# Prompt attention whose results stay in channel rows, with row factors applied in the merge

## The chip, the core and the metric

The kernel runs on one core of a Trainium2 chip. The metric is the device time of one execution in microseconds (us), start to end, for one step of a decoder layer on a prompt of 2048 tokens and 8 sequences of 8 new tokens each. PE is the matrix engine (PEld its weight loads), DVE the vector engine, ACT the scalar engine, POOL the general engine, SP the engine whose queue issues most transfers. PSUM is the memory that PE writes to, in 8 banks of 512 floats per partition; SBUF is the large on-chip memory of 128 partitions.

## The reference, cut to what matters

A layer normalises its input, projects it once, runs two token mixers side by side (a retention and a latent attention), multiplies each by a gate, projects both, adds them under two more gates and projects once more. The part that the change touches is the latent attention of the prompt and what follows it:

```python
def attend(args):
    qblk, start = args
    s = jnp.einsum('bqhd,bkhd->bhqk', qblk, k).astype(jnp.float32) * scale
    s = jnp.where(kpos[None, :] <= qpos[:, None], s, -jnp.inf)
    p = jax.nn.softmax(s, axis=-1).astype(v.dtype)
    return jnp.einsum('bhqk,bkhv->bqhv', p, v)
...
mla_o = mla_mixer(q_nope, q_pe, c_kv, k_pe, w_uk, w_uv) * jax.nn.silu(g_m)
p_mla = mla_o @ w_br_mla
merged = jax.nn.sigmoid(mg_r) * p_ret + jax.nn.sigmoid(mg_m) * p_mla
y = x + merged @ w_out
```

There are 8 heads with 64 value channels each (512 channels in all), 2048 positions, and query tiles of 128 rows. The softmax divides each row by the sum of its exponentials; that division can be done before or after the product with the values.

## The kernel before

The program has four stages, one after the other: `front` (projections and retention), `decode` (the new tokens), `attend` (prompt attention) and `merge` (gates, the two branch projections, the output projection, the norm). Every float is carried as a high and a low part for PE (`hi`, `lo`), and a product takes three matmuls (`three`, L66 to L68). All engines run their own hand-written list of instructions and wait for each other on counting semaphores; nothing is reordered.

**`attend`.** The loop goes over pairs of heads, and in a pair over 16 steps, 64 steps in all. A step handles two query tiles, a short one (`e` = 0) and a long one (`e` = 1), which together always have 17 blocks of 128 keys; the blocks are handled in 5 groups of up to 4. Step `g` works on three steps at once: scores of step `g`+1, transposes and most value products of step `g`, and the last two groups of values of step `g`-1. A group goes through these stages:

- `scores(j)` (PE): the product of queries and keys into bank j, plus the causal mask (L1881) on the diagonal block.
- `peak(j)` (DVE, L1812): the row maximum of the group; after a tile's last group, the maximum over its groups (L1816) and its negative (L1819, `nm`).
- `exps` (ACT, L1767): the exponentials, with their row sums in `total`.
- `turn(j)` (PE, L1889): the transposes, into bank 5 or 6.
- `high(j)` (ACT, L1754) and `low(j)` (DVE, L1802): the two parts of the transposed block, back into SBUF.
- `values(g, j)` (PE, L1900): values times probabilities into bank 7. The weights are the high and the low part of the values side by side (128 rows), and the moving data the high and the low part of the probabilities (256 columns). So bank 7 holds, for each of the two tiles, four partial sums: two halves of the partitions times two halves of the columns.

The four partial sums are added by PE. When `values(g-1, 4)` is done, ACT copies bank 7 into `ot` (L1773, "oc"); `folded()` multiplies it with a stacked identity (`fold`, L1910), which adds the partitions and turns the result to rows of tokens; DVE multiplies that with the reciprocals of the row sums (`result()`, L1837) into `out`. The row sums are added and inverted in `sums()` (L1826, L1829) in each step. `values(g, 0)`, the first to write to bank 7 again, waits for `result()`. SP stores `out` once per pair of heads to `OA` in DRAM (L1724), in rows of tokens. POOL has a task of its own: it loads the branch weights in 8 pieces and splits them into high and low parts (L1739 to L1743), as fast as they come.

PE's list for a step is, with the lines of the calls left out: scores(0), values(g-1,3), scores(1), values(g-1,4), turn(0), scores(2), turn(1), folded(), scores(3), turn(2), values(g,0), values(g,1), scores(4), turn(3), values(g,2), turn(4). DVE's: peak(0), peak(1), sums(), low(0), peak(2), result(), low(1), peak(3), low(2), peak(4), low(3), low(4). ACT's: oc, high(0), high(1), exps of tile 0, high(2), high(3), the first exps of tile 1, high(4), the other exps.

**`merge`.** It goes over 8 blocks of 256 tokens (the last also takes the 64 new tokens). SP's `main(n)` loads the inputs of block n into single buffers, as soon as the branch products of block n-1 are done. `turn(n)` (PE, L2171) transposes the block of `OA` back into channels, 8 transposes into banks 0 and 1; DVE multiplies them with the gate (`gated`, L2128), ACT and DVE split the product (L2092, L2130) into `ao`. For blocks after the first this runs between the first and the second token tile of the output projection of the block before. The branch products then take, for each of 8 channel groups k, 12 matmuls of the retention branch and 12 of the attention branch; only the latter need `ao`. In block 0 the output weights are still loaded and split on the way (L2105, L2144).

Of the kernel before, what the change touches and what calls it, by code (L numbers as in the profile page):

```python
# [1631 lines left out]
def attend(nc, T, early):  # L1632
# [7 lines left out]
    with ExitStack() as ctx:  # L1640
        sb, ps, sem = kit(nc, ctx)
        ident, hide, one_r = sb("t_ident", [P, P]), sb("t_hide", [P, P], F32R), sb("t_one_r", [P, P], F32R)
        hide_raw = sb("t_hide_raw", [P, P])
# [6 lines left out]
        total, den, rinv = sb("t_total", [P, 2, NGR]), sb("t_den", [P, 2, 2]), sb("t_rinv", [P, 2, 2])  # L1650
        ot = sb("t_ot", [P, 2, 2 * P])
        fold = sb("t_fold", [P, VD])
        out = sb("t_out", [P, 2, TILES, 2 * VD])
        w_raw = sb("t_w_raw", [P, 1, D_MODEL])
        bk = ps("t_bank", [P, 8, 512])
# [5 lines left out]
        by_group, by_tile, by_step = "qk mxs ex tp hi lo".split(), "red nm".split(), "dn rc pv oc of out".split()  # L1661
# [4 lines left out]
        w_in, w_high, w_low = sem("t_w_in"), sem("t_w_high"), sem("t_w_low")  # L1666
        block = ctx.enter_context(nc.Block())
# [23 lines left out]

        def over(eng, step):
# [11 lines left out]
        def _(sp):  # L1704
# [3 lines left out]
            sp.dma_start(hide_raw[:], T["hide"]).then_inc(consts, 16)  # L1708
# [11 lines left out]
            def store(r):  # L1720

                step_done(sp, "out", r, PAIR - 1)
                c = ds(2 * VD * r, 2 * VD)
                sp.dma_start(T["OA"][:, c].rearrange("(t p) n -> p t n", p=P), out[:, r % 2]).then_inc(stored, 16)  # L1724

            load(0)
            for r in range(1, NH // 2):
                load(r)
                store(r - 1)
            store(NH // 2 - 1)  # L1730
            sp.wait_ge(stored, 16 * (NH // 2))

        @block.gpsimd
        def _(g):
            g.wait_ge(consts, 32)
            g.tensor_copy(hide[:], hide_raw[:]).then_inc(ready, 1)
            g.tensor_copy(one_r[:], ident[:]).then_inc(ready, 1)
            for i, (w, src, c) in enumerate(early):
                g.dma_start(w_raw[:], T[src][c * P:(c + 1) * P, :].rearrange("(a p) n -> p a n", p=P)).then_inc(w_in, 16)  # L1739
                g.wait_ge(w_in, 16 * i + 16)  # L1740
# [3 lines left out]
                g.wait_ge(w_low, i + 1)  # L1744

        @block.scalar
        def _(a):
            def step(r, g, first, mid, last):
# [510 lines left out]
```

## Time and profile before

| what | us |
|---|---|
| median of 3 runs (2715.28 to 2720.17) | 2719.64 |
| the profiled execution | 2721.65 |
| its span, first to last instruction | 2719.9 |
| `front` and `decode`, to the start of `attend`'s transfers | 1722 |
| `attend`, first scores to the last result | 1746 to 2290 |
| `merge`, first transfer to the end | 2297 to 2720 |
| PE busy over the span | 2543.8 (94%) |
| DVE busy | 1462.3 (54%) |
| ACT busy | 1082.5 (40%) |
| POOL busy | 580.2 (21%) |

The profiled execution took 2721.65 us, of which 1.75 lie outside its span; it is 2.0 us above the median. Busy shares over the whole span mix stages with different limits. A row of the timeline has the start in us, the length, the engine, the line, what it writes and reads, and in brackets how long the engine had been idle before it and what it then waited for. Consecutive rows of one engine may overlap by a little, because a next instruction starts while the last one drains.

### The profile page before, as it was taken

How to read it: one execution, taken by the hardware profiler on the slowest of the kernel's cores; microseconds unless marked ns; L12 is line 12 of the kernel's file. 1: busy time of each engine (PE TensorE's matmuls, PEld its weight loads, DVE VectorE, ACT ScalarE, POOL GpSimd, SP SyncE). 2: the span in 40 equal slices, each digit the busy share in tenths (PEclk: the TensorE clock that was granted, in tenths of full speed). 3: DMA queues.
4: the chain of work that ended last, by engine and by line, in shares of the span. 5: the costliest groups of instructions: out<-in, count | busy, mean ns of one | idle time of the engine just before them, and what ended most of it. 6: DMA issues, size and time to landing. Idle time of an engine off the chain costs nothing. (4 is left out here: it accounts for less than half of the span.)

```text
span 2719.9 us, 44356 instructions
## 1 busy us (share of the span) xinstructions
PE 2543.8 (94%) x15981; PEld 2257.6 (83%) x15981; DVE 1462.3 (54%) x2772; ACT 1082.5 (40%) x2351; POOL 580.2 (21%) x446
## 2 busy tenths in 40 slices
PE   6999999999999999999789998499999997899998
PEld 6999987788878887788678887488888886799987
DVE  3345543355434554355368887288888885323232
ACT  3234331234313433233256664177777774211111
POOL 0023212124002320124115555130000000232322
PEclk9999999999999999999889998599999998899999
DMA  6677765778667876567344340632333202443431
GB/s 178 190 192 219 207 203 166 201 213 228 207 197 199 225 214 184 155 179 205 106 176 131 124 132 1 162 80 70 79 69 82 69 15 87 155 155 125 158 120 56
DMA packets 470443, 402.20 MB, mean 148 GB/s; under 512 B 50577, under 2 KB 419346, under 8 KB 463058
## 3 DMA queue, kind: packets, MB, share of 16 engines
q1 hardware_dynamic: 466690, 386.51, 50.2%
q10 hardware_dynamic: 2384, 8.65, 0.9%
q0 software_dynamic: 1152, 4.19, 0.5%
q8 instruction: 129, 2.11, 0.3%
q14 instruction: 88, 0.72, 0.1%
HBM read 297.82 MB, written 139.18 MB: 161 GB/s over the span
## 5 line engine op out<-in xcount | busy, mean ns | idle before, releaser
L66 PE MATMUL a_bank<-a_h_hi,a_w_hi 128*128 128x512 f32 (+3 forms) x1680 | 608.8, 362 | 20.8 <-DVE a_w_lo L755 15.8
L68 PE MATMUL a_bank<-a_h_hi,a_w_lo 128*128 128x512 f32 (+3 forms) x1680 | 596.4, 355 | 0.0
L67 PE MATMUL a_bank<-a_h_lo,a_w_hi 128*128 128x512 f32 (+3 forms) x1680 | 596.3, 355 | 0.0
L66 PEld LDWEIGHTS a_bank<-a_h_hi,a_w_hi 128*128 128x128 f32 (+1 forms) x1680 | 315.9, 188 | 67.8 <-DVE a_w_lo L755 19.0
L68 PEld LDWEIGHTS a_bank<-a_h_hi,a_w_lo 128*128 128x128 f32 (+1 forms) x1680 | 315.4, 188 | 44.3
L572 ACT ACTIVATE a_w_hi<-a_w_raw 128x1024 fp32r<-128x1024 f32 x168 | 175.0, 1043 | 436.7 <-PE a_bank L68 278.1
L67 PEld LDWEIGHTS a_bank<-a_h_lo,a_w_hi 128*128 128x128 f32 (+1 forms) x1680 | 316.1, 188 | 38.8
L755 DVE TENSOR_TENSOR a_w_lo<-a_w_raw,a_w_hi 128x1024 fp32r<-128x1024 f32 x168 | 205.7, 1225 | 207.5 <-ACT a_w_hi L572 207.5
L1802 DVE TENSOR_TENSOR t_pt<-t_bank,t_pt 128x512 fp32r<-128x512 f32 (+3 forms) x320 | 195.0, 610 | 73.0 <-ACT t_pt L1754 70.5
L1754 ACT ACTIVATE t_pt<-t_bank 128x512 fp32r<-128x512 f32 (+3 forms) x320 | 171.2, 536 | 134.8 <-PE t_bank L1889 134.2
L1767 ACT ACTIVATE t_prob<-t_bank,t_nm 128x512 f32<-128x512 f32 (+3 forms) x320 | 197.1, 628 | 37.3 <-DVE t_nm L1819 36.3
L1812 DVE TENSOR_REDUCE t_mx<-t_bank 128x1 f32<-128x512 f32 (+3 forms) x320 | 192.2, 604 | 36.4 <-PE t_bank L1881 28.7
L1900 PE MATMUL t_bank<-t_pt,t_vt 128*128 128x256 f32 x1088 | 190.1, 299 | 7.5 <-DVE t_pt L1802 6.3
L1309 POOL TENSOR_TENSOR p_nat<-p_lat,p_nat 128x1024 fp32r<-128x1024 f32 x64 | 152.2, 2378 | 152.9 <-DVE p_nat L1395 152.9
L1889 PE MATMUL t_bank<-t_ident,t_prob 128*128 128x128 f32 x1088 | 172.5, 274 | 0.2 <-DVE t_pt L1802 0.2
L768 DVE COPY a_zo<-a_bank 128x512 f32<-128x512 f32 (+2 forms) x90 | 53.7, 597 | 216.9 <-PE a_bank L68 216.9
L1900 PEld LDWEIGHTS t_bank<-t_pt,t_vt 128*128 128x128 f32 x1088 | 146.1, 189 | 28.0 <-DVE t_pt L1802 22.6
L66 PE MATMUL t_bank<-t_kt,t_qt 96*128 96x512 f32 (+3 forms) x320 | 133.1, 416 | 32.1 <-DMA t_vt<-between_VS 30.6
L1889 PEld LDWEIGHTS t_bank<-t_ident,t_prob 128*128 128x128 f32 x1088 | 129.5, 141 | 17.6 <-issue 0.7
L493 POOL TENSOR_TENSOR m_zs<-m_zs,m_sin 128x1024 f32<-128x1024 f32 (+1 forms) x17 | 39.5, 2325 | 409.0 <-DMA m_cs<-in_cs_pe 409.0
L67 PE MATMUL t_bank<-t_kt,t_qt 96*128 96x512 f32 (+3 forms) x320 | 118.2, 369 | 0.0
L68 PE MATMUL t_bank<-t_kt,t_qt 96*128 96x512 f32 (+3 forms) x320 | 118.1, 369 | 0.0
(322 smaller groups left out, 5327.2 us busy)
## 6 DMA issues: line engine op xcount, KB each, us to landing
a_w_raw<-in_w_in SPq DMA_DIRECT2D x164, 512.0 KB, 4.4
between_zT<-a_zo SPq DMA_DIRECT2D x164, 256.0 KB, 3.7
between_LAT<-in_lat_pool SPq DMA_DIRECT2D x256, 128.0 KB, 2.5
p_lat<-between_LAT SPq DMA_DIRECT2D x64, 512.0 KB, 3.1
y_mg<-between_zT SPq DMA_DIRECT2D x112, 128.0 KB, 2.5
t_qt<-between_QT SPq DMA_DIRECT2D x16, 768.0 KB, 12.6
a_x<-in_x_prompt SPq DMA_DIRECT2D x16, 512.0 KB, 5.6
m_zt<-between_zT SPq DMA_DIRECT2D x16, 512.0 KB, 4.5
```

Of the source, the lines that this page charges most:

```text
L66: pe.matmul(out, lh, rh, start=start, stop=False)
L67: pe.matmul(out, lh, rl, start=False, stop=False)
L68: return pe.matmul(out, ll, rh, start=False, stop=stop)
L572: a.activation(w_hi[:, i % 2, :, 0:m], w_raw[:, i % 2, :, 0:m], ACT.Copy).then_inc(w_his, 1)
L755: v.tensor_tensor(w_lo[:, i % 2, :, 0:m], w_raw[:, i % 2, :, 0:m], w_hi[:, i % 2, :, 0:m].bitcast(F32), ALU.subtract).then_inc(w_los, 1)
L1309: g.tensor_tensor(nat[t % 3][1][0:rows, 0:n], src, nat[t % 3][0][0:rows, 0:n].bitcast(F32), ALU.subtract).then_inc(S["nl"], 1)
L1754: a.activation(pt[:, c % 4, 0:n, 0], bk[:, 5 + c % 2, 0:n * P].rearrange("p (m q) -> p m q", q=P), ACT.Copy).then_inc(S["hi"], 1)
L1767: a.activation(prob[:, s, j, 0:n], bk[:, j, 0:n], ACT.Exp, bias=nm[:, s, e:e + 1], scale=SCALE, accum_out=total[:, s, j:j + 1]).then_inc(S ...
L1802: v.tensor_tensor(pt[:, c % 4, 0:n, 1], bk[:, 5 + c % 2, 0:n * P].rearrange("p (m q) -> p m q", q=P), pt[:, c % 4, 0:n, 0].bitcast(F32), A ...
L1812: v.tensor_reduce(mx[:, s, j:j + 1], bk[:, j, 0:n * P], AX.X, ALU.max).then_inc(S["mxs"], 1)
L1889: i = p.transpose(bk[:, 5 + c % 2, m * P:(m + 1) * P], prob[:, g % 2, j, m * P:(m + 1) * P], ident[:])
L1900: i = p.matmul(bk[:, 7, 2 * P * e:2 * P * (e + 1)], vt[u][:, k0 + m], pt[:, c % 4, m].rearrange("p x q -> p (x q)"), start=(k0 + m == 0), ...
```

## The change

In `attend` the results stay in channel rows. `folded()` and its matmuls go. ACT copies only that half of bank 7's partitions which belongs to the other part of the values, into the partitions where the head's results shall lie (64 partitions, all 512 columns). DVE's `result()` adds bank 7's own half to it, in place (64 x 512), and now `values(g, 0)` waits for this addition ("ad"). POOL adds the two halves of the columns into `out` (64 x 256), one addition in every step. The output has channels as rows and is stored to `OAT`.

The row sums stay in a table for all heads and tiles (`total`, set to zero by POOL at the start). `sums()` goes from the steps; in the last full step DVE adds the whole table at once, PE transposes it, DVE inverts it, and SP stores the factors to `RINV`.

POOL's loading and splitting of the branch weights is spread: it issues a piece in step 4, 8, 12, ... and splits it one step later, instead of one after the other from the start.

In `merge` the 8 transposes of a block, their identity and its load go. SP loads the block of `OAT` with channels as rows, and two more transfers spread the row factors of the two heads of each channel group over 64 partitions each (`scale`, which lies in the buffer of `ao_lo`). DVE multiplies twice, the result with the gate and the product with the factors, both from SBUF.

```diff
-        fold = sb("t_fold", [P, VD])
...
+            def step(r, g_, first, mid, last):
+                if last:
...
+                    step_done(g, "ad", r, g_ - 1)
...
+                    g.tensor_tensor(out[rows, r % 2, k:TILES - k:TILES - 1 - 2 * k], ot[rows, :, 0], ot[rows, :, 1],
+                                    ALU.add).then_inc(S["out"], 1)
+                    step_done(g, "out", r, g_ - 1)
+                i, m = divmod(PAIR * r + g_ - 4, 4)
+                if 0 <= i < len(early) and m == 0:
+                    fetch(i)
+                elif 0 <= i < len(early) and m == 1:
+                    split(i)
...
                 if last:
                     step_done(a, "pv", r, g - 1)
-                    step_done(a, "of", r, g - 2)
-                    a.activation(ot[:].rearrange("p e q -> p (e q)"), bk[:, 7], ACT.Copy).then_inc(S["oc"], 1)
+                    step_done(a, "out", r, g - 2)
+                    a.activation(ot[half_rows(g - 1)].rearrange("p e x q -> p (e x q)"), bk[half_rows(g - 1, True), 7],
+                                 ACT.Copy).then_inc(S["oc"], 1)
...
                 def result():
-                    b, k = (g - 1) % 2, (g - 1) % HS
-                    u = (g - 1) % PAIR // HS
-                    step_done(v, "of", r, g - 1)
...
+                    rows = half_rows(g - 1)
+                    step_done(v, "oc", r, g - 1)
+                    both = ot[rows].rearrange("p e x q -> p (e x q)")
+                    v.tensor_tensor(both, bk[rows, 7], both, ALU.add).then_inc(S["ad"], 1)
...
                     if j == 0:
-                        step_done(p, "out", r, g - 1)
+                        step_done(p, "ad", r, g - 1)
...
-                def folded():
-
-                    step_done(p, "oc", r, g - 1)
-                    for e in range(2):
-                        for x in range(2):
-                            i = p.matmul(bk[:, 7, 2 * P + VD * e:2 * P + VD * (e + 1)], ot[:, e, x * P:(x + 1) * P], fold[:],
-                                         start=(x == 0), stop=(x == 1))
-                    i.then_inc(S["of"], 1)
...
+                if mid and not first:
+                    p.wait_ge(added, 1)
+                    p.transpose(bk[:, 0, 0:P], den[:], ident[:]).then_inc(flipped, 1)
...
-                sp.dma_start(oa[:], T["OA"][p0, :].rearrange("(a p) n -> p a n", p=P)).then_inc(main_in, 16)
+                sp.dma_start(oa[:], T["OAT"][:, p0].rearrange("(k p) t -> p k t", p=P)).then_inc(main_in, 16)
+                for e in range(2):
+                    each = T["RINV"].rearrange("(k e) t -> e k t", e=2)[e:e + 1, :, p0]
+                    sp.dma_start(scale[VD * e:VD * e + VD], each.to_broadcast([VD, FC, W])).then_inc(main_in, 16)
...
-                v.wait_ge(main_in, 64 * n + 64)
-                at(v, "turn", n)
+                v.wait_ge(main_in, 96 * n + 96)
                 at(v, "aol", n - 1)
-                v.tensor_tensor(gm[:], bk[:, 0:2].rearrange("p a (c t) -> p (a c) t", c=2), gm[:], ALU.mult).then_inc(S["gated"], 1)
+                v.tensor_tensor(gm[:], oa[:], gm[:], ALU.mult).then_inc(S["opened"], 1)
+                at(v, "opened", n)
+                v.tensor_tensor(gm[:], gm[:], scale, ALU.mult).then_inc(S["gated"], 1)
```

How this stands in the engines' lists is shown at two places. First DVE, from the last `peak` before `low(0)` to `low(2)` of one step. Before (the L1826 and L1829 rows are `sums()`, L1837 is `result()`, L1802 `low`, L1812 `peak`):

```order
L1812 TENSOR_REDUCE t_mx<-t_bank 128x1
L1826 TENSOR_REDUCE t_den<-t_total 128x1 x2
L1829 RECIPROCAL t_rinv<-t_den 128x2
L1802 TENSOR_TENSOR t_pt<-t_bank,t_pt 128x3x128
L1812 TENSOR_REDUCE t_mx<-t_bank 128x1
L1837 TENSOR_TENSOR t_out<-t_bank,t_rinv 128x2x64
L1802 TENSOR_TENSOR t_pt<-t_bank,t_pt 128x4x128
```

The same stretch of DVE with the change (L1836 is now `low`, L1846 `peak`, L1859 `result()`):

```order
L1846 TENSOR_REDUCE t_mx<-t_bank 128x1
L1836 TENSOR_TENSOR t_pt<-t_bank,t_pt 128x3x128
L1846 TENSOR_REDUCE t_mx<-t_bank 128x1
L1859 TENSOR_TENSOR t_ot<-t_bank,t_ot 64x512
L1836 TENSOR_TENSOR t_pt<-t_bank,t_pt 128x4x128
```

Three small instructions ahead of `low(0)` are gone, and between `peak(2)` and `low(1)` an operation over 512 columns stands where one over 128 stood. Second PE, from `turn(1)` to `scores(4)` of one step, before (L1889 is `turn`, L1910 the fold, L1900 `values`):

```order
L1889 MATMUL t_bank<-t_ident,t_prob 128x128 x4
L1910 MATMUL t_bank<-t_fold,t_ot 128x64 x4
L66 MATMUL t_bank<-t_kt,t_qt 128x512
L67 MATMUL t_bank<-t_kt,t_qt 128x512
L68 MATMUL t_bank<-t_kt,t_qt 128x512
L1889 MATMUL t_bank<-t_ident,t_prob 128x128 x4
L1900 MATMUL t_bank<-t_pt,t_vt 128x256 x7
```

and with the change (L1914 is `turn`, L1925 `values`):

```order
L1914 MATMUL t_bank<-t_ident,t_prob 128x128 x4
L66 MATMUL t_bank<-t_kt,t_qt 128x512
L67 MATMUL t_bank<-t_kt,t_qt 128x512
L68 MATMUL t_bank<-t_kt,t_qt 128x512
L1914 MATMUL t_bank<-t_ident,t_prob 128x128 x4
L1925 MATMUL t_bank<-t_pt,t_vt 128x256 x7
```

The four fold matmuls are gone and nothing else has moved; `values(g, 0)` and `values(g, 1)` (the x7) stand right behind `turn(2)` as before.

## Rows read from the trace of the kernel before

**Rows 1.** Stretches: busy PE, PEld, DVE, ACT, POOL; PE clock, DMA share, GB/s.

```profile
1764.00:1830.00 66.00, 65.14 (x469) 59.00 (x468) 53.98 (x143) 47.54 (x126) 23.38 (x17) 1.00 0.25 70
1830.00:1896.00 66.00, 65.14 (x469) 58.80 (x467) 54.25 (x144) 47.55 (x128) 0.00 (x0) 1.00 0.28 63
...
2360.00:2400.00 40.00, 40.00 (x271) 36.93 (x270) 12.59 (x16) 5.56 (x11) 12.33 (x17) 1.00 0.44 145
...
2279.00:2289.00 10.00, 7.84 (x59) 6.62 (x57) 4.65 (x11) 5.79 (x15) 0.00 (x0) 1.00 0.01 2
```

**Rows 2.** Timeline of one attention step, from oc to the values.

```profile
1839.37 0.63 ACT L1773 ACTIVATE t_ot<-t_bank 128x512 f32<-128x512 f32 x1
...
1840.41 0.56 DVE L1802 TENSOR_TENSOR t_pt<-t_bank,t_pt 128x384 fp32r<-128x384 f32 x1 [0.21 <-ACT t_pt L1754]
...
1840.57 1.00 PE L1910 MATMUL t_bank<-t_fold,t_ot 128*128 128x64 f32 x8
1840.77 0.60 ACT L1754 ACTIVATE t_pt<-t_bank 128x512 fp32r<-128x512 f32 x1 [0.39 <-PE t_bank L1889]
1840.88 0.68 DVE L1812 TENSOR_REDUCE t_mx<-t_bank 128x1 f32<-128x512 f32 x1
...
1841.38 0.47 PE L66 MATMUL t_bank<-t_kt,t_qt 96*128 96x512 f32 x1
...
1841.61 0.29 DVE L1837 TENSOR_TENSOR t_out<-t_bank,t_rinv 128x128 f32<-128x128 f32 x1
...
1841.82 0.68 DVE L1802 TENSOR_TENSOR t_pt<-t_bank,t_pt 128x512 fp32r<-128x512 f32 x1
...
1842.50 1.08 PE L1900 MATMUL t_bank<-t_pt,t_vt 128*128 128x256 f32 x7
```

**Rows 3.** Timeline: low(0) and the values of two more steps.

```profile
1848.72 0.69 DVE L1802 TENSOR_TENSOR t_pt<-t_bank,t_pt 128x512 fp32r<-128x512 f32 x1 [0.56 <-ACT t_pt L1754]
...
1850.65 1.19 PE L1900 MATMUL t_bank<-t_pt,t_vt 128*128 128x256 f32 x8
...
1881.79 0.69 DVE L1802 TENSOR_TENSOR t_pt<-t_bank,t_pt 128x512 fp32r<-128x512 f32 x1 [0.34 <-ACT t_pt L1754]
...
1883.99 1.20 PE L1900 MATMUL t_bank<-t_pt,t_vt 128*128 128x256 f32 x8
```

**Rows 4.** Transfers while attention starts: queue, packets, MB, share of 16 engines (24 us).

```profile
q0 software_dynamic: 144, 0.52, 9.9%
```

**Rows 5.** Attention's last copy and result, a POOL addition in merge, the last store.

```profile
2287.46 0.60 ACT L1773 ACTIVATE t_ot<-t_bank 128x512 f32<-128x512 f32 x1 [1.11 <-PE t_bank L1900]
...
2289.25 0.29 DVE L1837 TENSOR_TENSOR t_out<-t_bank,t_rinv 128x128 f32<-128x128 f32 x1 [2.54 <-PE t_bank L1910]
...
2315.35 0.74 POOL L2079 TENSOR_TENSOR y_mm<-y_mm 128x256 f32<-128x256 f32 x1 [19.35 <-DVE y_mm L2139]
...
between_OA<-t_out SPq DMA_DIRECT2D x1, 1024.0 KB, 5.0
```

**Rows 6.** Merge's first block: timeline rows, then two stretches as in rows 1.

```profile
2305.81 1.94 PE L2171 MATMUL y_bank<-y_ident,y_oa 128*128 128x128 f32 x8 [16.60 <-DMA y_gm<-between_zT]
...
2310.20 1.23 DVE L2130 TENSOR_TENSOR y_ao_lo<-y_gm,y_ao_hi 128x1024 fp32r<-128x1024 f32 x1 [1.12 <-ACT y_ao_hi L2092]
...
2299.00:2303.00 4.00, 0.00 (x0) 0.00 (x0) 0.00 (x0) 0.00 (x0) 0.00 (x0) 0.50 1.04 360
...
2307.00:2315.00 8.00, 6.83 (x32) 6.54 (x31) 2.94 (x3) 1.06 (x1) 0.00 (x0) 0.50 0.56 216
```

**Rows 7.** Merge's transposes: block 1 (timeline), block 2 (chain that ended last).

```profile
2358.57 1.09 PE L2171 MATMUL y_bank<-y_ident,y_oa 128*128 128x128 f32 x8 [1.36 <-DMA y_gm<-between_zT]
...
2403.91 0.87 PE y_bank L2171 x8
...
2407.87 1.22 DVE L2128 TENSOR_TENSOR y_gm<-y_bank,y_gm 128x1024 f32<-128x1024 f32 x1
...
2415.54 0.28 PE L66 MATMUL y_bank<-y_ro_hi,y_wr_hi 128*128 128x256 f32 x1
```

More of the change, by code:

```diff
@@ L1666, in attend @@
         w_in, w_high, w_low = sem("t_w_in"), sem("t_w_high"), sem("t_w_low")
+        added, flipped, inverted = sem("t_added"), sem("t_flipped"), sem("t_inverted")
         block = ctx.enter_context(nc.Block())
@@ L1690, in of_tile, with half_rows @@
             return js[0], js[-1] + 1
+        def half_rows(g, other=False):
+            u = g % PAIR // HS ^ other
+            return slice(VD * u, VD * u + VD)
         def over(eng, step):
@@ L1729, in _, with fetch, split @@
                 store(r - 1)
+            sp.wait_ge(inverted, 1)
+            sp.dma_start(T["RINV"].rearrange("h (t q) -> (h t) q", q=P), rinv[:]).then_inc(stored, 16)
             store(NH // 2 - 1)
-            sp.wait_ge(stored, 16 * (NH // 2))
+            sp.wait_ge(stored, 16 * (NH // 2 + 1))
         @block.gpsimd
         def _(g):
+            g.memset(total[:], 0.0).then_inc(ready, 1)
             g.wait_ge(consts, 32)
-            g.tensor_copy(hide[:], hide_raw[:]).then_inc(ready, 1)
+            g.tensor_copy(hide[:], hide_raw).then_inc(ready, 1)
             g.tensor_copy(one_r[:], ident[:]).then_inc(ready, 1)
-            for i, (w, src, c) in enumerate(early):
+            def fetch(i):
+                w, src, c = early[i]
+                if i:
+                    g.wait_ge(w_low, i)
+                else:
+                    g.wait_ge(ready, 3)
                 g.dma_start(w_raw[:], T[src][c * P:(c + 1) * P, :].rearrange("(a p) n -> p a n", p=P)).then_inc(w_in, 16)
+            def split(i):
+                w, src, c = early[i]
                 g.wait_ge(w_in, 16 * i + 16)
@@ L1744, in _ @@
                 g.wait_ge(w_low, i + 1)
+            def step(r, g_, first, mid, last):
+                if last:
+                    k = (g_ - 1) % HS
+                    rows = half_rows(g_ - 1)
+                    step_done(g, "ad", r, g_ - 1)
+                    if r >= 2 and g_ == 1:
+                        g.wait_ge(stored, 16 * (r - 1))
+                    g.tensor_tensor(out[rows, r % 2, k:TILES - k:TILES - 1 - 2 * k], ot[rows, :, 0], ot[rows, :, 1],
[6 more added lines that the diff above has]
+                    split(i)
+            over(g, step)
         @block.scalar
@@ L1787, in step @@
                     exps(1, 1)
+            a.wait_ge(ready, 1)
             over(a, step)
@@ L1844, in step @@
                 if mid:
-                    sums()
                     low(0)
@@ L1927, in step @@
                     turn(1)
-                if last:
-                    folded()
                 if first:
@@ L1970, in merge @@
         bk = ps("y_bank", [P, 8, 512])
-        per = dict(turn=1, gated=1, aoh=1, aol=1, br=DC, mul=DC, add=DC, mh=DC, ml=DC, y=4, res=4, sq=2, mean=2, rs=2, fin=2)
+        per = dict(opened=1, gated=1, aoh=1, aol=1, br=DC, mul=DC, add=DC, mh=DC, ml=DC, y=4, res=4, sq=2, mean=2, rs=2, fin=2)
         CR = {k: 2 * n for k, n in per.items()}
         S = {k: sem("y_" + k) for k in per}
-        consts, gained, wh, wl, halved = (sem("y_" + x) for x in "consts gained wh wl halved".split())
+        gained, wh, wl, halved = (sem("y_" + x) for x in "gained wh wl halved".split())
         wload = [sem(f"y_wl{x}") for x in range(2)]
@@ L2202, in _ @@
                         i.then_inc(S["y"], 1)
-                    if a == 0 and n + 1 < NB:
-                        turn(n + 1)
 def hybrid_step(nc, T):
```

67 lines of the change are left out of this document (23 added, 44 removed).

## The prediction, made before the run

> **What bounds the kernel now.** The chain that ended last covers only part of the span, so I read by stages. In attention PE is busy 65.14 of 66 us, with POOL at work beside it and without, and DVE for 54; in merge PE is busy 40.00 of 40 [rows 1]. Read alone, that says that whatever PE loses is gained. So I looked at one attention step in order of time, for what would be late next if PE were early.
>
> In that step [rows 2] ACT copies bank 7 (oc, 1839.37) and then makes high(0); DVE has been idle for 0.21 us when high(0) lets it start low(0) at 1840.41. From there DVE runs on: peak(2) at 1840.88, result() at 1841.61 (it had to wait for the end of the fold), low(1) at 1841.82 to 1842.50. PE folds from 1840.57 to 1841.38, then does scores(3), turn(2) and, from 1842.50, the seven value matmuls, of which the first three are values(0). Values(1) needs low(1). It came to it some 0.35 us after low(1) was done: that is all the slack there is.
>
> **The change in attention.** *Removed on PE*: the fold, a slot of 1841.38 - 1840.57 = 0.81 us [rows 2], 64 times 52 us. *Added on DVE*: result() now goes over 512 columns instead of 128. No row shows this very form; the nearest is low(1), also PSUM and SBUF in, SBUF out, 512 columns: 0.68 us. An operation of DVE that waits for nothing starts about 0.08 before the end of the one ahead (1841.61 + 0.29 against 1841.82 [rows 2]), so 0.60 from start to start; the other end would be 0.29, the old form, or 0.68 + 0.06 if it drains first. I take 0.60. *Removed on DVE*: sums(), which stood ahead of low(0), where DVE waits for ACT anyway [rows 2, 3]. Worth nothing. ACT's copy takes half the partitions but the same 512 columns; I keep 0.6 us.
>
> So values(1) of this step can start at: low(0) 1840.41, + 0.47 to peak(2), + 0.60 to result(), + 0.60 to low(1), + 0.69 for low(1), + 0.05 to PE = 1842.82. Before, it started at 1842.50 + 3 x 0.115 = 1842.85 (seven matmuls, the last ending 1.08 after the first, some 0.115 apart [rows 2]). The difference is -0.03 us: **PE, freed from the fold, waits 0.8 us for DVE instead.** (Values(0), which waits for the addition, is free at 1842.2 and is not the later one here.)
>
> Does low(0) itself come earlier? It hangs on high(0), that on the copy oc, that on the end of values(4) and on ACT's exponentials, and all of them on PE's work behind values(1): scores(4), the maxima, the next turns and scores. PE does it without a gap before [rows 1], so it moves with values(1) and no faster. A step is then a loop through PE, ACT and DVE, not a queue on PE.
>
> I did the same sum for the eight steps of one head, which differ in the sizes of their groups. They come to +0.11, -0.03, +0.15, +0.13, -0.05, -0.14, -0.12 and +0.13 us. The third (low(0) at 1848.72 + 3 x 0.60 + 0.69 + 0.05 = 1851.26, against 1850.65 + 4 x 0.115 = 1851.11) and the seventh (1884.33 against 1884.45) can be followed in [rows 3]. The sum is +0.18 per head, **+1.5 us** for all. An error of 0.1 us in each step makes 6.
>
> *POOL* gets an addition over 64 x 256 in each step; the nearest row is 128 x 256, 0.74 us [rows 5]. Only ACT's next copy waits for it, most of a step later. Behind it on POOL's queue stand the splits of the weights: even one that waits a whole step for its transfer is done before that copy. Its use of SBUF beside DVE costs nothing that can be seen: DVE's busy time is 53.98 with POOL's splits and 54.25 without [rows 1]. Zero.
>
> *Start*: the first piece of branch weights no longer shares the engines with the first heads' loads, for which PE waits. Its packets took 9.9% of 24 us = 2.4 us of all 16 engines [rows 4]; I take **-2.0**, with 0 and -2.4 as ends.
>
> *End*: from the last copy (2287.46 + 0.60) to the last result took 1.48 us, through the fold [rows 5]. Now it is DVE 0.68 + POOL at most 0.74 + two handovers of 0.06: 1.54. **Zero.** The table of row sums is added, turned and inverted before that. The inversion of 128 columns has no row; DVE waits 2.54 us in front of its last result [rows 5], so up to that it is hidden.
>
> *Store*: the last one, 1 MB in rows of 512 B, took 5.0 us [rows 5]; at the 360 GB/s of merge's first loads [rows 6] it would be 2.9 plus a latency. In rows of 8 KB: **-0.7**, ends 0 and -2.1. The Trainium skill (DMA: Bandwidth & Descriptors, Specifications) puts the least transfer for line rate at 512 B; by that this term would be 0 and the sum 0.7 higher, but 1 MB in 5.0 us is slower than what the next loads reach.
>
> **The change in merge.** *First block*: two transfers of 0.26 MB each stand ahead of the gate's: 0.52 MB at 360 GB/s [rows 6] = 1.4 us, less 0.4 for the identity's issue. So the inputs are complete 1.0 later, at 2306.8. Then two multiplications of 1.23, 1.12 for ACT's copy, 1.23 for the low part and handovers: 2311.7, against 2310.20 + 1.23 = 2311.43 [rows 6]. PE, which began with transposes, begins 1.0 later and is at a granted clock of 0.50 (1.2 GHz) up to 2315 [rows 6]; its rise may come later too. Together **+1.0**, ends 0 and +3. *Blocks 1 to 7*: block 1's transposes waited 1.36 us for the gate's transfer and took 0.87, the other six 0.87 each [rows 7]: -2.2 and -5.2, **-7.4**. The second multiplication hides: DVE starts the gating at 2407.87, needs some 4.8 instead of 3.6 us for the chain, and PE asks for it after 2415.54 [rows 7].
>
> **Sum**: +1.5 - 2.0 - 0.7 + 1.0 - 7.4 = -7.6. From the profiled execution's 2721.65: 2714.0; from the median: **2712.0 us**.
>
> **The rivals.** *A, the forecast*: own range 2704 to 2720.
>
> *B, the fold's time comes back*: PE's share [rows 1] speaks for it. Then +1.5 becomes -52 (2658.7 us), or about half (2685). It would need low(0) or the handovers on DVE to come sooner than the rows show.
>
> *C, DVE's chain is longer than I made it, and the kernel slower*. The new result() reads what ACT wrote and is written in place; if it starts only when peak(2) has drained, and low(1) only when it has, each with a handover, the two cost 0.28 us more: 63 x 0.28 = +17.6, so 2729.6 us. The place is DVE between low(0) and low(1). It decides from 0.21 us per step: all else is -9.1, and +5.4 would need 14.5 / 63 = 0.23. Against it: handovers from low to peak and from result() to low(1) do overlap before [rows 2].
>
> *D, the clock falls*: PE now waits in each step. A step takes 8.31 us from low(0) to low(0) [rows 2, 3], 7.5 without the fold; if the clock fell to half for a tenth of that, a step would gain 0.75 us, some 0.5 of it on the loop: 63 x 0.5 = 32, so 2743 us. Against it: at attention's end PE is idle for 22% of 10 us at a granted clock of 1.00 [rows 1]. The Trainium skill (TensorE: Matmul & The Clock Gate, A second HAM failure mode: psum-queue depth-cycling) tells of a kernel in which short idle times between groups of matmuls made the clock go back and forth; the row mentioned does not agree.
>
> *E, POOL is late*: it holds up ACT's copy in some steps, a few us in all; 2718.
>
> **How the numbers follow.** A 0.70, B 0.08, C 0.14, D 0.03, E 0.05. A measurement of this kernel can tell 0.2% (5.4 us) from no change, so faster is below 2714.2 and slower above 2725.0. Of A 0.43 is faster, 0.26 same and 0.01 slower; B is faster; of C 0.02 is same and 0.12 slower; D is slower; of E 0.01 is faster and 0.04 same. Faster 0.52, same 0.32, slower 0.16. The range takes in A, the nearer part of C and the upper edge of B: 2695 to 2729.
>
> **What would show it.** In the trace after, PE idles 0.3 to 1 us in nearly each attention step in front of its value matmuls, and the releaser is DVE's result() or low(1); PE's busy share there falls to some 90%, DVE's stays near 82%. Result() takes 0.68 us and low(1) starts 0.60 after it. The 64 steps together take as long as before, within 6 us. In merge, blocks follow 0.87 us closer. I am wrong if the steps get shorter by 0.2 us or more (low(0) then hangs on something else), or longer with DVE's gaps between peak(2) and low(1).

## The result, and the profile after

The changed kernel took 2736.8 us (median of 4 runs, 2734.11 to 2737.87) against 2717.47 us for the kernel before in the same comparison: 1.0071 times as long, 95% interval 1.0055 to 1.0087. It is 19.3 us slower; 2712.0 us had been forecast, 7.6 us below the median known then, and the time lies above the range. The profiled execution took 2734.11 us with a span of 2732.3 us. In it the stages ahead of attention, which the change does not touch, are 7.8 us shorter than in the profile of before (over the profiles of all kernels here, none of which touches them, they end between 1714.4 and 1724.3 us), so I compare stage by stage.

Attention first: the first copy oc and the last one, before (two rows) and after (two rows).

```profile
1764.43 0.61 ACT L1773 ACTIVATE t_ot<-t_bank 128x512 f32<-128x512 f32 x1
...
2287.46 0.60 ACT L1773 ACTIVATE t_ot<-t_bank 128x512 f32<-128x512 f32 x1 [1.11 <-PE t_bank L1900]
```

```profile
1754.06 0.59 ACT L1809 ACTIVATE t_ot<-t_bank 64x512 f32<-64x512 f32 x1
...
2300.37 0.59 ACT L1809 ACTIVATE t_ot<-t_bank 64x512 f32<-64x512 f32 x1 [1.41 <-PE t_bank L1925]
```

There are 63 steps between them: 523.03 us before, 546.31 after, so **8.30 and 8.67 us for a step, +23.3 us in all**. From attention's first transfer to the first oc it is 42.3 before and 39.6 after (-2.6); from the last oc to merge's first transfer 9.3 and 8.2 (-1.2); merge 423.1 and 423.8 (+0.7). The sum is +20.2.

The stretches of [rows 1] after, with the same columns, in attention and in merge:

```profile
1764.00:1830.00 66.00, 59.33 (x390) 49.44 (x389) 52.37 (x116) 46.17 (x121) 10.59 (x12) 1.00 0.26 62
1830.00:1896.00 66.00, 59.03 (x382) 48.71 (x381) 52.08 (x113) 46.89 (x124) 13.13 (x13) 1.00 0.27 65
2390.00:2430.00 40.00, 40.00 (x258) 36.84 (x258) 12.25 (x17) 6.40 (x13) 12.84 (x18) 0.97 0.56 167
```

In attention PE is now busy for 59 of 66 us at the same granted clock of 1.00, and DVE did not get busier. In the waits of 1760 to 2310 (engine, what waited, for whom: us in total, times, longest) PE waits for the addition in nearly every step:

```profile
PE t_bank L1925 <- DVE t_ot L1859: 38.2, 61, 0.7
```

One step of the second head of a pair, which answers to [rows 2], in order of time:

```profile
1831.69 0.59 ACT L1809 ACTIVATE t_ot<-t_bank 64x512 f32<-64x512 f32 x1
...
1832.31 1.19 ACT L1789 ACTIVATE t_pt<-t_bank 128x384 fp32r<-128x384 f32 x2
1832.84 0.56 DVE L1836 TENSOR_TENSOR t_pt<-t_bank,t_pt 128x384 fp32r<-128x384 f32 x1 [0.80 <-ACT t_pt L1789]
...
1833.31 0.68 DVE L1846 TENSOR_REDUCE t_mx<-t_bank 128x1 f32<-128x512 f32 x1
...
1834.02 0.69 DVE L1859 TENSOR_TENSOR t_ot<-t_bank,t_ot 64x512 f32<-64x512 f32 x1
...
1834.75 0.69 DVE L1836 TENSOR_TENSOR t_pt<-t_bank,t_pt 128x512 fp32r<-128x512 f32 x1
...
1834.86 1.01 PE L1925 MATMUL t_bank<-t_pt,t_vt 128*128 128x256 f32 x4 [0.70 <-DVE t_ot L1859]
...
1835.49 0.19 PEld L1925 LDWEIGHTS t_bank<-t_pt,t_vt 128*128 128x128 f32 x1 [0.25 <-DVE t_pt L1836]
```

The order is the predicted one: low(0), peak(2), result(), low(1), values. PE stands first in front of values(0) for the addition, then the weights of values(1) wait for low(1), which here ends last. The distances are not the predicted ones. From peak(2) to result() it is 0.71 us and from result() to low(1) 0.73, where 0.60 was taken twice: each operation starts 0.03 to 0.04 us **after** the end of the one ahead, not 0.08 before it. From oc to high(0) it is 0.62 us, where before a copy of 128 rows let high(0) begin after 0.48. In a step of the first head of a pair, DVE's three operations follow each other as predicted:

```profile
1903.71 0.68 DVE L1846 TENSOR_REDUCE t_mx<-t_bank 128x1 f32<-128x512 f32 x1
...
1904.31 0.67 DVE L1859 TENSOR_TENSOR t_ot<-t_bank,t_ot 64x512 f32<-64x512 f32 x1
...
1904.91 0.67 DVE L1836 TENSOR_TENSOR t_pt<-t_bank,t_pt 128x512 fp32r<-128x512 f32 x1
```

In merge, the first block's inputs came 14.6 us after the first issue (2308.52), before 9.0. The transfers' rates in 40 slices of 2300 to 2322 us, then attention's last store, the load of the row factors, and DVE at the first and second block:

```profile
GB/s 0 0 118 1 0 0 462 417 372 417 238 0 0 0 0 0 0 48 102 333 374 382 385 358 343 357 345 210 130 67 84 73 60 56 110 188 277 367 374 378
...
between_OAT<-t_out SPq DMA_DIRECT2D x1, 1024.0 KB, 3.8
...
y_ao_lo<-between_RINV SPq DMA_DIRECT2D x2, 256.0 KB, 8.7
...
2323.16 1.23 DVE L2146 TENSOR_TENSOR y_gm<-y_oa,y_gm 128x1024 f32<-128x1024 f32 x1 [21.46 <-DMA y_gm<-between_zT]
...
2382.97 1.28 DVE L2178 SCALAR_TENSOR_TENSOR y_x<-y_x,y_rstd,y_fgain 128x1024 f32<-128x1024 f32 x1 [7.56 <-DMA y_fgain<-in_final_norm_gain]
2384.17 1.22 DVE L2146 TENSOR_TENSOR y_gm<-y_oa,y_gm 128x1024 f32<-128x1024 f32 x1
```

While the row factors are spread (by their place in the queue) the rate falls to 56 to 130 GB/s. Later the norm gain, also one row spread over partitions, comes late, DVE waits 7.56 us for it, and block 1's gating stands behind. The squares of blocks 0, 1 and 2 show what each block takes, before:

```profile
2357.97 1.06 ACT L2110 ACTIVATE y_mm<-y_x 128x1024 f32<-128x1024 f32 x1 [12.61 <-DVE y_x L2152]
...
2404.67 1.06 ACT L2110 ACTIVATE y_mm<-y_x 128x1024 f32<-128x1024 f32 x1 [9.62 <-DVE y_x L2152]
...
2449.77 1.06 ACT L2110 ACTIVATE y_mm<-y_x 128x1024 f32<-128x1024 f32 x1 [9.62 <-DVE y_x L2152]
```

and after:

```profile
2374.07 1.06 ACT L2129 ACTIVATE y_mm<-y_x 128x1024 f32<-128x1024 f32 x1 [12.39 <-DVE y_x L2172]
...
2423.55 1.06 ACT L2129 ACTIVATE y_mm<-y_x 128x1024 f32<-128x1024 f32 x1 [9.62 <-DVE y_x L2172]
...
2467.74 1.06 ACT L2129 ACTIVATE y_mm<-y_x 128x1024 f32<-128x1024 f32 x1 [9.61 <-DVE y_x L2172]
```

From the first issue (2296.76 and 2308.52) to block 0's square 61.2 us became 65.6 (+4.3); from block 0 to block 1 46.7 became 49.5 (+2.8); from block 1 to block 2, and so on to block 6, 45.1 became 44.2 (-0.9); to the longer last block 60.2 became 57.9 (-2.3).

### The profile page after: what moved, and what is told of

Its sections match the earlier page's. It is cut to its first block and busy times, and to the rows that moved or that the text cites. A ratio compares the mean times of both kernels' runs of the same rounds, so it can differ in the third digit from the quotient of the medians.

```text
span 2732.3 us, 43067 instructions
## 1 busy us (share of the span) xinstructions
PE 2504.4 (92%) x15406; PEld 2189.8 (80%) x15406; DVE 1478.6 (54%) x2588; ACT 1089.5 (40%) x2351; POOL 628.7 (23%) x511
## 5 line engine op out<-in xcount | busy, mean ns | idle before, releaser
L1836 DVE TENSOR_TENSOR t_pt<-t_bank,t_pt 128x512 fp32r<-128x512 f32 (+3 forms) x320 | 194.2, 607 | 92.3 <-ACT t_pt L1789 89.1
L1925 PE MATMUL t_bank<-t_pt,t_vt 128*128 128x256 f32 x1088 | 197.6, 302 | 48.9 <-DVE t_ot L1859 38.8
L1925 PEld LDWEIGHTS t_bank<-t_pt,t_vt 128*128 128x128 f32 x1088 | 148.8, 189 | 87.9 <-issue 52.0
L1846 DVE TENSOR_REDUCE t_mx<-t_bank 128x1 f32<-128x512 f32 (+3 forms) x320 | 192.2, 604 | 45.2 <-PE t_bank L1906 35.9
L1914 PE MATMUL t_bank<-t_ident,t_prob 128*128 128x128 f32 x1088 | 173.9, 275 | 8.0 <-DVE t_pt L1836 3.4
L66 PE MATMUL t_bank<-t_kt,t_qt 96*128 96x512 f32 (+3 forms) x320 | 133.5, 417 | 29.7 <-DMA t_vt<-between_VS 28.2
L1770 POOL TENSOR_TENSOR t_out<-t_ot 64x256 f32<-64x256 f32 x64 | 46.7, 730 | 482.9 <-DVE t_ot L1859 474.3
L1914 PEld LDWEIGHTS t_bank<-t_ident,t_prob 128*128 128x128 f32 x1088 | 124.2, 141 | 40.4 <-issue 25.1
L493 POOL TENSOR_TENSOR m_zs<-m_zs,m_sin 128x1024 f32<-128x1024 f32 (+1 forms) x17 | 39.6, 2327 | 409.6 <-DMA m_cs<-in_cs_pe 409.6
L67 PE MATMUL t_bank<-t_kt,t_qt 96*128 96x512 f32 (+3 forms) x320 | 118.2, 369 | 0.0
```

What stands on the lines that cost most here:

```text
L66: pe.matmul(out, lh, rh, start=start, stop=False)
L67: pe.matmul(out, lh, rl, start=False, stop=False)
L1836: v.tensor_tensor(pt[:, c % 4, 0:n, 1], bk[:, 5 + c % 2, 0:n * P].rearrange("p (m q) -> p m q", q=P), pt[:, c % 4, 0:n, 0].bitcast(F32), A ...
L1846: v.tensor_reduce(mx[:, s, j:j + 1], bk[:, j, 0:n * P], AX.X, ALU.max).then_inc(S["mxs"], 1)
L1914: i = p.transpose(bk[:, 5 + c % 2, m * P:(m + 1) * P], prob[:, g % 2, j, m * P:(m + 1) * P], ident[:])
L1925: i = p.matmul(bk[:, 7, 2 * P * e:2 * P * (e + 1)], vt[u][:, k0 + m], pt[:, c % 4, m].rearrange("p x q -> p (x q)"), start=(k0 + m == 0), ...
```

## The experiments

All kernels are the changed one with the edit shown; "..." marks what is left out of an edit. Several of them add other rows and so leave out the right attention results; the expectation in front of each says so. "Step" is the mean of the 63 distances from oc to oc in the profile, and behind it the mean in the steps of the first and of the second head of a pair; the ratio is to the kernel before, with its 95% interval.

| kernel | step us | first / second head | ratio |
|---|---|---|---|
| before | 8.30 | 8.36 / 8.25 | 1 |
| changed | 8.67 | 8.62 / 8.73 | 1.0071 (1.0055 to 1.0087) |
| both operations on 128 rows | 8.36 | 8.41 / 8.31 | 1.0012 (1.0001 to 1.0023) |
| addition on 128 rows | 8.57 | 8.62 / 8.51 | 1.0053 (1.0036 to 1.0070) |
| copy on 128 rows | 8.46 | 8.40 / 8.52 | 1.0027 (1.0015 to 1.0040) |
| copy of 64 rows, no shift | 8.55 | 8.39 / 8.72 | 1.0053 (1.0035 to 1.0071) |
| both in partitions 0 to 63 | 8.32 | 8.37 / 8.27 | 0.9994 (0.9981 to 1.0007) |
| both in partitions 32 to 63 | 8.76 | 8.81 / 8.71 | 1.0102 (1.0085 to 1.0119) |
| both in two pieces of 256 columns | 8.81 | 8.73 / 8.89 | one run alone |
| additions on POOL | 7.74 | 7.77 / 7.71 | 0.9878 (0.9861 to 0.9894) |

### Which operations lose their overlap

**Both whole.**

```diff
-                    a.activation(ot[half_rows(g - 1)]..., bk[half_rows(g - 1, True), 7], ACT.Copy)
+                    a.activation(ot[:]..., bk[:, 7], ACT.Copy)
-                    both = ot[rows]...; v.tensor_tensor(both, bk[rows, 7], both, ALU.add)
+                    both = ot[:]...; v.tensor_tensor(both, bk[:, 7], both, ALU.add)
```

> ScalarE's copy takes all 128 rows of bank 7 into the same 128 rows, and VectorE's addition runs over all 128 rows; the rest of the changed kernel is as it is, so the attention results are other sums (rows are added to themselves instead of to the other half). Theory: an operation on 64 partitions starts its successor only after its own whole duration (0.59 us on ScalarE, 0.69 us on VectorE, then 0.03 us), one on 128 partitions lets it start 0.08 to 0.12 us before its end; both lie on the loop, so each step gets back about 0.15 us (copy to first high) and 0.24 us (peak(2) to result, result to low(1)), 0.39 times 63 = 24 us: about 2712 us, attention 543 us instead of 566. Rival (it is the addition in place, or the chain of semaphores copy-addition-values itself, whatever the rows): no change, 2737 us.

2721.89 us. The overlap is back (0.60, 0.60 and 0.48 us) and the rival falls: an addition in place, behind the copy's semaphore, loses no overlap by itself. A step got 0.31 us back, not 0.39: VectorE had lost something in only half of the steps, as the next two kernels show.

**Each alone: the addition, then the copy on 128 rows.** (One of the two edits above.)

> Only VectorE's addition runs over 128 rows (in place, as in the changed kernel); ScalarE's copy keeps its 64 shifted rows. The 64 rows that are not used gather sums that nobody reads; GpSimd clears the tile once ahead. Theory (64 rows cost the overlap): peak(2) to result 0.60 us and result to low(1) 0.60 us instead of 0.71 and 0.73, so 0.24 times 63 = 15 us back: about 2722 us. Rival (in place or the wait for the copy): 2737 us, both distances unchanged.

> Only ScalarE's copy takes all 128 rows, unshifted; VectorE's addition keeps its 64 rows (and adds a row to itself, so the sums are others). Theory: copy to first high 0.47 us instead of 0.62, 0.15 times 63 = 9.5 us back: about 2727 us, if that distance lies on the loop in every step. Rival: the loop goes through VectorE alone and ScalarE has slack there: 2737 us.

2731.99 and 2726.44 us. The whole addition changes nothing in the first head's steps (8.62) and takes 0.21 us from the second head's. The whole copy takes 0.21 and 0.22 us from both heads'. So VectorE lost its overlap only where rows 64 to 127 were added, though both heads add 64 rows: "64 rows cost the overlap" is wrong.

**Copy without shift.**

```diff
-                    ... bk[half_rows(g - 1, True), 7], ACT.Copy)
+                    ... bk[half_rows(g - 1), 7], ACT.Copy)
```

> ScalarE's copy keeps 64 rows, but takes the rows that it writes to instead of the other 64 (no shift between partitions); the sums are others. Theory (the number of rows costs the overlap): nothing changes, copy to first high stays 0.62 us, 2737 us. Rival (the shift to other partitions costs it): 0.47 us, about 2727 us.

2729.48 us. Neither expectation holds as a whole: the first head's steps are as short as with everything whole (8.39), the second's unchanged (8.72). DVE and ACT in a step of the first head:

```profile
1774.50 0.68 DVE L1846 TENSOR_REDUCE t_mx<-t_bank 128x1 f32<-128x512 f32 x1
1775.10 0.67 DVE L1859 TENSOR_TENSOR t_ot<-t_bank,t_ot 64x512 f32<-64x512 f32 x1
1775.70 0.67 DVE L1836 TENSOR_TENSOR t_pt<-t_bank,t_pt 128x512 fp32r<-128x512 f32 x1
...
1772.79 0.59 ACT L1809 ACTIVATE t_ot<-t_bank 64x512 f32<-64x512 f32 x1
1773.27 0.59 ACT L1789 ACTIVATE t_pt<-t_bank 128x512 fp32r<-128x512 f32 x1
```

and of the second:

```profile
1833.99 0.68 DVE L1846 TENSOR_REDUCE t_mx<-t_bank 128x1 f32<-128x512 f32 x1
1834.70 0.70 DVE L1859 TENSOR_TENSOR t_ot<-t_bank,t_ot 64x512 f32<-64x512 f32 x1
1835.43 0.69 DVE L1836 TENSOR_TENSOR t_pt<-t_bank,t_pt 128x512 fp32r<-128x512 f32 x1
...
1832.37 0.59 ACT L1809 ACTIVATE t_ot<-t_bank 64x512 f32<-64x512 f32 x1
1832.99 1.20 ACT L1789 ACTIVATE t_pt<-t_bank 128x384 fp32r<-128x384 f32 x2
```

The same instruction on the same number of rows: 0.60 and 0.60, or 0.71 and 0.73; 0.48 or 0.62. What differs is the partition at which it begins.

**Both in partitions 0 to 63, then 32 to 63.**

```diff
-                    rows = half_rows(g - 1)
+                    rows = half_rows(0)        # then: slice(32, 64)
-                    ... ot[half_rows(g - 1)], bk[half_rows(g - 1, True), 7], ACT.Copy
+                    ... ot[half_rows(0)], bk[half_rows(0), 7], ACT.Copy        # then: slice(32, 64) twice
```

> ScalarE's copy and VectorE's addition stay at 64 rows, but both always work in partitions 0 to 63 (unshifted), and GpSimd reads its sums there; the sums of the odd heads are others. In the runs before, the steps of the first head of a pair (addition in partitions 0 to 63) had peak(2) to result 0.60 us, those of the second (partitions 64 to 127) 0.71. Theory: an operation that touches partitions from 64 on lies badly beside neighbours that begin at partition 0, whatever its number of rows; so here copy to first high is 0.48 us and both distances of the addition 0.60 us in both heads, 8.36 us for a step as with 128 rows, about 2722 us. Rival (64 rows of 128 cost the overlap): 0.62 and 0.71, 8.67 us for a step, 2737 us.

> ScalarE's copy and VectorE's addition both take 32 rows, partitions 32 to 63, in both heads (GpSimd clears the tile once ahead); half of each sum is left out, so the attention results are others. It asks where the lost overlap begins. Theory A (it is lost by operations that touch partitions from 64 on): as with partitions 0 to 63, copy to first high 0.48 us, peak(2) to addition 0.60 us, about 8.3 us for a step, 2718 to 2722 us. Theory B (it is lost by any operation that does not begin at partition 0, beside neighbours that do): 0.62 and 0.71 us in both heads, 8.7 us for a step, 2737 us or a little more.

2718.45 us with partitions 0 to 63: no time lost. 2743.99 us with 32 to 63, where both heads lose (8.81 and 8.71 against 8.37 and 8.27). So it is not the upper half, but any beginning other than partition 0, beside neighbours that begin there. One step with partitions 32 to 63:

```profile
1825.27 0.68 DVE L1847 TENSOR_REDUCE t_mx<-t_bank 128x1 f32<-128x512 f32 x1
1825.98 0.68 DVE L1860 TENSOR_TENSOR t_ot<-t_bank,t_ot 32x512 f32<-32x512 f32 x1
1826.69 0.69 DVE L1837 TENSOR_TENSOR t_pt<-t_bank,t_pt 128x512 fp32r<-128x512 f32 x1
```

**Two pieces right behind each other.** Is it the beginning itself, or that it differs from the neighbour's?

```diff
+                    for e in range(2):
+                        both = ot[rows, e]...
+                        i = v.tensor_tensor(both, bk[rows, 7, 2 * P * e:2 * P * e + 2 * P], both, ALU.add)
...                  # and ScalarE's copy likewise
```

> The changed kernel with ScalarE's copy and VectorE's addition each cut into two operations of 256 columns, one right behind the other in the same partitions; nothing is left out. Operations of 128x256 take 0.42 us on VectorE and 0.38 on ScalarE in these traces. Theory A (an operation waits for the end of the one ahead when it begins in other partitions than that one): only the first piece, and the operation behind the second, wait; the second piece starts 0.08 us before the first ends on VectorE and 0.12 before it on ScalarE, so the pair takes about 0.76 us and 0.65 us also in partitions 64 to 127. Theory B (any operation that does not begin at partition 0 is without overlap): the second piece starts 0.03 us after the first ends, the pair takes 0.87 us on VectorE in the second head of a pair and 0.79 on ScalarE. The whole: some 0.1 us more in each step by A, about 2744 us, some 0.2 by B, about 2750.

One run took 2747.99 us, beside one of the kernel before at 2724.9; between the two expected times, 2744 and 2750, it cannot decide, but the trace can. DVE in a step of the second head (the pair is the x2), then ACT:

```profile
1992.94 0.68 DVE L1848 TENSOR_REDUCE t_mx<-t_bank 128x1 f32<-128x512 f32 x1
1993.65 0.77 DVE L1862 TENSOR_TENSOR t_ot<-t_bank,t_ot 64x256 f32<-64x256 f32 x2
1994.45 0.69 DVE L1838 TENSOR_TENSOR t_pt<-t_bank,t_pt 128x512 fp32r<-128x512 f32 x1
...
1982.23 0.64 ACT L1810 ACTIVATE t_ot<-t_bank 64x256 f32<-64x256 f32 x2
1982.90 1.14 ACT L1789 ACTIVATE t_pt<-t_bank 128x384 fp32r<-128x384 f32 x2
```

The pair takes 0.77 and 0.64 us, though a piece takes 0.42 and 0.37 by itself: the second piece overlaps the first, though both begin at partition 64. The change of the beginning costs, on both sides of the pair; theory A holds for both engines.

### Whether DVE's chain held the fold's time

```diff
-                    a.activation(ot[half_rows(g - 1)]..., bk[half_rows(g - 1, True), 7], ACT.Copy)
+                    a.activation(ot[:]..., bk[:, 7], ACT.Copy)
...
-                if last: result()
...
-                        step_done(p, "ad", r, g - 1)
+                        step_done(p, "oc", r, g - 1)
...
-                    g.tensor_tensor(out[...], ot[rows, :, 0], ot[rows, :, 1], ALU.add)
+                    g.tensor_tensor(to, ot[other, :, 0], ot[other, :, 1], ALU.add)
+                    for x in range(2):
+                        g.tensor_tensor(to, to, ot[rows, :, x], ALU.add)
```

> ScalarE copies all 128 rows of bank 7 unshifted, the values of the next step wait for this copy alone, and GpSimd makes the sum with three additions of 64x256 (0.73 us each); VectorE has no addition left. Theory (the loop goes through VectorE's low(0), peak(2), addition, low(1), so that the fold could not be gained): without the addition a step is up to 0.60 us shorter than the 8.36 us with 128 rows, about 7.8 us, times 63 = 35 to 38 us under that kernel: 2685 us; if TensorE's own work ends last before that, up to 2700. Rival (VectorE's place is taken by the peaks or by ScalarE's exponentials, which end last anyway): 8.3 us for a step, 2718 us. Rival (three additions on GpSimd come too late for the copy of the next step): ScalarE waits for t_out, over 2722 us.

2687.27 us, 0.9878 of the kernel before (0.9861 to 0.9894): **faster than both**. A step is 7.74 us, 0.62 below the kernel with both operations whole; that is about the start-to-start time of result(), 0.60. Two things go together in this edit, result()'s place ahead of low(1) and the wait of values(0) for the addition; they were not taken apart. POOL stays ahead: ACT waits for it once, 0.4 us. The stretches of [rows 1] again:

```profile
1764.00:1830.00 66.00, 64.56 (x435) 55.86 (x435) 52.76 (x121) 51.81 (x139) 22.28 (x28) 1.00 0.26 64
1830.00:1896.00 66.00, 64.12 (x433) 55.26 (x431) 52.54 (x118) 50.59 (x134) 27.99 (x32) 1.00 0.40 96
```

PE is busy for 64 of 66 us again, now without the fold.

### The merge's first two blocks

**Row factors from distinct rows.**

```diff
-                    each = T["RINV"].rearrange("(k e) t -> e k t", e=2)[e:e + 1, :, p0]
-                    sp.dma_start(scale[VD * e:VD * e + VD], each.to_broadcast([VD, FC, W]))
+                    each = T["OAT"].rearrange("(k e p) t -> e p k t", e=2, p=VD)[e, :, :, p0]
+                    sp.dma_start(scale[VD * e:VD * e + VD], each)
```

> The merge's two loads of row factors read, in the same pieces of 1 KB, 64 different rows of the attention's results instead of the same four rows 64 times, so the merge multiplies by other numbers; the attention is that of the changed kernel. Theory (reading the same rows 64 times is what slows these two transfers to 60 to 100 GB/s): they run at about 360 GB/s, the inputs of the first block are there about 10 us after the first issue instead of 14.6, the norm gain's wait before block 1 falls too: 4 to 7 us back, about 2731 us. Rival (the number of pieces and of queued transfers does it): 14.6 us again, 2737 us.

2732.07 us, 1.0047 (1.0030 to 1.0063), not clearly apart from the changed kernel. The trace tells more; 40 slices of 2310 to 2322 us and DVE's first operation (first issue at 2311.66):

```profile
GB/s 0 0 0 0 0 0 0 0 0 58 61 126 294 379 386 386 379 389 382 372 352 355 338 355 345 345 355 167 164 174 205 259 229 219 201 184 218 297 345 348
...
2322.97 1.23 DVE L2146 TENSOR_TENSOR y_gm<-y_oa,y_gm 128x1024 f32<-128x1024 f32 x1 [18.13 <-DMA y_gm<-between_zT]
```

The two loads run at 164 to 259 GB/s instead of 56 to 130, and the inputs are there after 11.3 us instead of 14.6. Reading one row for many partitions is thus the larger part of the 5.6 us; but 360 GB/s is not reached, and what holds the rest stays open. Block 1 gains too, though the norm gain is loaded as late in the queue as before. The squares of blocks 0 and 1, and DVE's wait for the norm gain between them:

```profile
2374.25 1.06 ACT L2129 ACTIVATE y_mm<-y_x 128x1024 f32<-128x1024 f32 x1 [12.57 <-DVE y_x L2172]
...
2418.47 1.06 ACT L2129 ACTIVATE y_mm<-y_x 128x1024 f32<-128x1024 f32 x1 [9.63 <-DVE y_x L2172]
...
2379.42 1.28 DVE L2178 SCALAR_TENSOR_TENSOR y_x<-y_x,y_rstd,y_fgain 128x1024 f32<-128x1024 f32 x1 [3.83 <-DMA y_fgain<-in_final_norm_gain]
```

From block 0 to block 1 it is 44.2 us, as from each block to the next behind them, against 46.5 to 51.0 in the nine profiles whose merge is that of the changed kernel. So it is the slow loads of the row factors, behind which the gate's inputs and the norm gain queue, that cost the +2.8; the next two kernels, which move the norm gain alone for block 1, do not get it back. The whole merge takes 415.1 us here, 8.0 less than before the change, where -6.4 had been forecast; in those nine profiles it takes 420.5 to 424.6.

**The loads on a second queue; the norm gain earlier.**

```diff
+            spread(a_, 0)        # the two loads of block 0, on ScalarE's queue
...
+                    sp.dma_start(fgain[:], ...)        # ahead of main(1)
                 if n < NB - 1:
                     main(n + 1)
```

> The first block's two loads of row factors are issued by ScalarE on its own queue, beside SyncE's other loads, and the norm gain is loaded ahead of block 1's inputs; the attention is that of the changed kernel. Theory (the slow transfers hold back what is queued behind them): the first block's inputs are there about 10 to 11 us after the first issue, the wait of 7.6 us for the norm gain is gone: 4 to 7 us back, about 2731 us. Rival (they slow all 16 engines whatever the queue): 14 us again, only the norm gain's part of about 3 us, 2734 us.

2737.85 us, 1.0075 (1.0051 to 1.0098): nothing gained. The rival holds for the first block: its inputs came 15.2 us after SP's first issue (2309.53 to 2324.72), since the other loads now ran beside the slow ones:

```profile
y_ao_lo<-between_RINV ACTq DMA_DIRECT2D x2, 256.0 KB, 6.8
y_ro_hi<-between_ROT SPq DMA_DIRECT2D x1, 512.0 KB, 9.7
```

The first of them lands after 9.7 us instead of 4.1. The part of 3 us that was expected from the norm gain did not come either: DVE no longer waits for it, but for block 1's inputs, 5.71 us, and from block 0's square to block 1's it is 48.4 us.

**POOL's additions with the norm gain ahead** (the two edits together, the row factors on SyncE's queue).

> The kernel with the whole copy on ScalarE and the three additions on GpSimd, and in the merge the norm gain is loaded ahead of the second block's inputs; the row factors stay on SyncE's queue. The attention's steps stay at 7.74 us. Theory (the wait of 7.6 us for the norm gain, which stands ahead of the second block's gating on VectorE, costs the 2.8 us by which the distance from block 0 to block 1 grew): 2687 minus 3 = 2684 us. Rival (the gain's transfer, which reads one row 128 times, now holds back the second block's inputs instead): 2687 us or up to 3 more.

2681.39 us, 0.9875 (0.9858 to 0.9891), and 7.76 us for a step. DVE's wait for the norm gain is gone, but it now waits for block 1's inputs:

```profile
2325.85 1.28 DVE L2171 SCALAR_TENSOR_TENSOR y_x<-y_x,y_rstd,y_fgain 128x1024 f32<-128x1024 f32 x1 [0.68 <-POOL y_rstd L2096]
2333.00 1.22 DVE L2139 TENSOR_TENSOR y_gm<-y_oa,y_gm 128x1024 f32<-128x1024 f32 x1 [5.86 <-DMA y_gm<-between_zT]
```

From block 0's square to block 1's it is 48.5 us, against 49.0 with the additions on POOL alone: one wait has taken the place of the other. That the time is near the theory's 2684 is luck, for its mechanism did not occur; the rival's did. As a whole the two kernels' intervals cover each other, so no gain is shown.

## Why the prediction was wrong

**The loop was right.** That PE, freed from the fold, would wait for DVE's low(0), peak(2), result(), low(1) is what the waits show (61 times in 63 steps, PE busy for 90%). One detail was off: values(0) is held up by the addition more than I had it, since PE begins it some 0.15 us after the addition's end, not 0.05. With both operations in partitions 0 to 63 the same change of the work gives 8.32 us a step; +1.5 us for all steps, 8.33, had been forecast. And with result() taken out of the chain a step fell from 8.30 to 7.74 us: 0.56 of the fold's 0.81 us did come.

**The step that failed** is the attention term, +1.5 us; it measured +23.3. Two of its sizes were wrong. First, "0.60 from start to start" for result(): true in the first head of a pair, 0.71 and 0.73 in the second. With the addition on 128 rows 0.21 us came back in the steps of the second head, 6.6 us in all. Second, the copy: I kept its 0.6 us and looked at nothing else, but it too begins in other partitions than its neighbours. High(0) starts 0.14 us later behind it, and it starts 0.15 us later itself in the 40 steps in which it follows the exponentials without waiting for PE. With the copy on 128 rows 0.21 us a step came back, in both heads, 13.5 us. With both operations in partitions 0 to 63 it was 0.35 us a step, 22.0 us, and that is the whole of the 21.8 us between forecast and measurement. I had read the overlap from operations that all begin at partition 0 and applied it to one that does not.

**Rival C** had DVE's place and kind (no overlap on either side of result(), 0.28 us a step) with the wrong cause, reading and writing in place, and it did not have ACT. It said 2729.6 us. B, D and E did not occur: in attention's steps PE's share fell and the fold's time did not come back, the granted clock stayed at 1.00, and ACT never waited for POOL.

The Trainium skill (VectorE: DVE Perf Modes, Two Vector instructions with no wait between them) gives, as a model, the rule that I passed over. A Vector instruction whose input or output begins in another group of 32 partitions than the one last read from, or written to, in the same memory starts only when all earlier ones have finished. The runs agree for VectorE: 0.60 us with partitions 0 to 63, 0.71 with 32 to 63 and with 64 to 127, and overlap again inside a pair. The section gives no price; with the 0.11 and 0.13 us measured here in half of the steps, the forecast would by that rule have been an estimated 7 to 8 us higher, about 2719 us. For ScalarE the runs above show it by themselves.

**The smaller terms.** Start: -2.0, measured -2.6, though in the other kernels with this start the same stretch took from 39.1 to 42.1 us, so its size is not sure. Store and end: -0.7, measured -1.2; the store landed after 3.8 us instead of 5.0 [rows 5]. Merge's later blocks: -0.87 each, measured -0.9, and -2.3 at the last. Merge's first block: +1.0 with an upper end of 3, measured +4.3, because I priced the row factors at the 360 GB/s of other loads [rows 6]. Block 1: -2.2, measured +2.8, for the same reason, which I did not have there at all: I had put the cost of its row factors at nothing. Of merge's -6.4 nothing was left; with row factors from distinct rows it was there. One slip of the sum changes nothing: eight times +0.18 is +1.4, not +1.5.

## What to carry to other kernels

Before moving work into part of the partitions, see at which partition each operation begins and at which its neighbours on that engine begin; a change cost a tenth of a microsecond and more on either side here, in every step whose chain ran through it. When work leaves a busy engine, walk the loop for what is late next and take that out as well: three additions on an engine with time to spare (POOL) were worth more than one on the loop. A load that spreads one row over many partitions should be priced from a row of its own kind, and with it whatever queues behind it: moving one of these loads ahead only moved the wait.

## What the runs showed of the hardware that I had not expected

- In these traces ScalarE and VectorE start an operation 0.08 to 0.15 us before the end of the one ahead if both begin in the same partitions, and 0.02 to 0.04 us after its end if they do not: VectorE 0.60 against 0.71 to 0.73 us for 512 columns, ScalarE 0.48 against 0.62. The number of rows made no difference: 64 rows from partition 0 went as 128 did, and 32 rows from partition 32 as 64 from partition 64.
- Loads that read one row of 1 KB for 64 partitions ran at 56 to 130 GB/s, and loads on another queue beside them were slowed too (9.7 us to landing instead of 4.1); pieces of the same size from distinct rows ran at 164 to 259.
- The last store of 1 MB took 3.8 us in rows of 8 KB against 5.0 in rows of 512 B.
